# Token tensor of the second block with rows of 1152 bytes instead of 1088

## What is computed

```
meta_b = jnp.broadcast_to(meta[None].astype(x.dtype), (B, N_META, D_MODEL))
h = jnp.concatenate([meta_b, x], axis=1)
u = rms_norm(h, g_pre_mix[l])
proj = u @ w_in[l]
z_pool, v_conv, g_conv, gate_a, gate_b = jnp.split(proj, splits, axis=-1)
y_a = causal_multiscale_pool(z_pool, w_grp[l], pool_scale[l]) @ w_pool_out[l]
y_b = conformer_conv(v_conv, g_conv, w_dw[l], b_dw[l],
                     conv_ln_g[l], conv_ln_b[l]) @ w_conv_out[l]
m = jax.nn.sigmoid(gate_a) * y_a + jax.nn.sigmoid(gate_b) * y_b
h = h + rms_norm(m @ w_o[l], g_post_mix[l])
```

## Time and profile before

| | us |
|---|---|
| median of the runs shown | 2025.81 |
| the profiled execution itself | 2026.39 |
| its span in the trace | 2024.6 |
| PE busy | 2013.1 |
| DVE busy | 1513.4 |
| ACT busy | 1016.1 |

### The profile page before, as it was taken

One profiled execution on the slowest core, in us unless ns is written; L12 is line 12 of the kernel. 1 busy time (PEld: TensorE's weight loads), 2 busy tenths in 40 slices (PEclk: granted clock), 3 DMA queues, 4 the chain that ended last, 5 costly groups with the idle time before them and its releaser, 6 DMA issues.

```text
span 2024.6 us, 28913 instructions
## 1 busy us (share of the span) xinstructions
PE 2013.1 (99%) x10488; PEld 1715.0 (85%) x10488; DVE 1513.4 (75%) x2051; ACT 1016.1 (50%) x1329; POOL 82.9 (4%) x91
## 2 busy tenths in 40 slices
PE   9999999999999999999999999999999999999998
PEld 7888898888888888999888888888888888888886
DVE  6766766566756655578999856588987997898896
ACT  6645444555544544433444644454563464365353
POOL 0000102001002000002000000000000000000001
PEclk9999999999999999999999999999999999999999
DMA  9687655655667656555666566655576467467563
GB/s 348 198 202 186 177 157 172 190 175 174 179 203 243 192 190 185 175 176 159 189 195 198 178 218 185 192 173 160 190 238 195 156 208 226 146 208 235 178 209 134
DMA packets 265477, 389.33 MB, mean 192 GB/s; under 512 B 12504, under 2 KB 147032, under 8 KB 264571
## 3 DMA queue, kind: packets, MB, share of 16 engines
q1 hardware_dynamic: 262587, 377.19, 61.1%
q0 software_dynamic: 2624, 10.54, 1.9%
q10 hardware_dynamic: 144, 0.01, 0.0%
HBM read 385.02 MB, written 2.54 MB: 191 GB/s over the span
## 4 chain that ended last, share of the span: by engine, by line
PE 98%; SPq 1%; DMA 1%; DVE 0%; ACT 0%; issue 0%; DVEq 0%
PE acc L705 18%; PE acc L682 17%; PE acc L683 17%; PE acc L684 17%; PE acc L703 10%; PE acc L696 2%; PE acc L695 2%; PE acc L697 2%; PE aux L734 1%; PE aux L736 1%; PE aux L735 1%; PE acc L701 1%; PE acc L734 1%; PE acc L736 1%; PE acc L735 1%; PE aux L1638 1%
## 5 line engine op out<-in xcount | busy, mean ns | idle before, releaser
L536 DVE TENSOR_TENSOR low_rows<-stage_rows,high_rows 128x1024 fp32r<-128x1024 f32 x494 | 585.8, 1202 | 267.1 <-ACT high_rows L521 260.4
L521 ACT ACTIVATE high_rows<-stage_rows 128x1024 fp32r<-128x1024 f32 x494 | 506.6, 1034 | 516.1 <-PE acc L684 441.4
L521 ACT ACTIVATE w_high<-stage 128x1024 fp32r<-128x1024 f32 (+1 forms) x264 | 276.1, 1047 | 395.2 <-PE acc L705 292.9
L536 DVE TENSOR_TENSOR w_low<-stage,w_high 128x1024 fp32r<-128x1024 f32 (+1 forms) x264 | 319.9, 1220 | 173.9 <-ACT w_high L521 169.5
L705 PE MATMUL acc<-u,w_high 128*128 128x512 f32 x900 | 248.0, 394 | 0.0
L705 PE MATMUL acc<-hT,w_high 128*128 128x512 f32 x645 | 177.5, 394 | 0.0
L705 PEld LDWEIGHTS acc<-u,w_high 128*128 128x128 f32 x900 | 152.9, 189 | 19.1
L703 PEld LDWEIGHTS acc<-u,w_low 128*128 128x128 f32 x960 | 146.8, 188 | 20.5
L703 PE MATMUL acc<-u,w_low 128*128 128x256 f32 x960 | 152.4, 281 | 0.0
L682 PE MATMUL acc<-high_rows,hT 128*128 128x512 f32 x384 | 151.8, 395 | 0.0
L684 PE MATMUL acc<-high_rows,hT 128*128 128x512 f32 x384 | 149.6, 390 | 0.0
(11 more groups left out here) (451 smaller groups left out, 3690.1 us busy)
## 6 DMA issues: line engine op xcount, KB each, us to landing
stage_rows<-in_w_in SPq DMA_DIRECT2D x160, 512.0 KB, 3.7
stage<-in_w_in SPq DMA_DIRECT2D x136, 512.0 KB, 3.6
stage_rows<-in_w_down SPq DMA_DIRECT2D x128, 512.0 KB, 4.4
stage<-in_w_up SPq DMA_DIRECT2D x120, 512.0 KB, 4.5
stage_rows<-in_w_o SPq DMA_DIRECT2D x64, 512.0 KB, 4.1
stage_rows<-in_w_pool_out SPq DMA_DIRECT2D x16, 512.0 KB, 3.9
stage_rows<-in_w_conv_out SPq DMA_DIRECT2D x16, 512.0 KB, 4.4
stage_rows<-in_w_mem_kv SPq DMA_DIRECT2D x14, 512.0 KB, 10.9
```

Source lines behind the costliest of these rows:

```text
L521: act.activation(high[:, pr, k_from:kt, 0:p.cols], src[:, slot, k_from:kt, 0:p.cols], ACT.Copy).then_inc(high_done, 1)
L536: dve.tensor_tensor(low[:, pr, k_from:kt, 0:p.cols], src[:, slot, k_from:kt, 0:p.cols], high[:, pr, k_from:kt, 0:p.cols].bitcast(F32), ALU ...
```

## The change

The tensor becomes `u_wide`, with rows of WIDE = 288 tokens, 1152 bytes (9 x 128), of which the last 16 are never used. It starts 2 KB earlier, so that it ends where `uT` ended. Held tokens now start on a multiple of 128 bytes in both halves; streamed tokens start 64 bytes past one in both halves.

The 2 KB in front belong to the last feature tile of `merged_pair`, which `w_o` reads to its end. The feature tiles are therefore rotated: tile 15 lies in place 0, tile k in place k + 1, and the meta tokens of tile 15 are written later than the others, just before x_low of q = 7 (in the first slab of `glu_in`), by two DVE instructions of their own. A small class `Wide` does the rotation, so that the rest of the code still says `uT`.

```diff
+WIDE = TM + 16
-        uT = at("uT", Z + 64.0625, [P, KT, 2, TM], F32R)
+        u_wide = at("u_wide", Z + 62.0625, [P, KT, 2, WIDE], F32R)
+        class Wide:
+            def __getitem__(self, at):
+                _, k, half, cols = at
+                return u_wide[:, (k + 1) % KT, half, cols]
+        uT = Wide()
-            return Part(A["w_in_2"], col0, full, lambda k: (uT[:, k, 0, :], uT[:, k, 1, :]), ("pair_ready", 16), width=TM, stride=stride)
+            return Part(A["w_in_2"], col0, full, lambda k: (uT[:, k, 0, 0:TM], uT[:, k, 1, 0:TM]), ("pair_ready", 16), width=TM, stride=stride)
                     for q in (2 * r, 2 * r + 1):
+                        if q == 7:
+                            dve.wait_ge(s("u_high"), 16)
+                            v = tmp[:, 0, (KT - 1) * META:KT * META]
+                            link(dve.tensor_copy(uT[:, KT - 1, 0, 0:META], v))
+                            link(dve.tensor_tensor(uT[:, KT - 1, 1, 0:META], v, uT[:, KT - 1, 0, 0:META].bitcast(F32), ALU.subtract))
                         low_scaled(uT, q, 2 + q % 2, META, "g_pre_mix_2", "u_high", 0)
-                    link(dve.tensor_copy(uT[:, :, 0, 0:META], v))
-                    dve.tensor_tensor(uT[:, :, 1, 0:META], v, uT[:, :, 0, 0:META].bitcast(F32), ALU.subtract).then_inc(s("meta_ready"), 1)
+                    first = v[:, 0:KT - 1, :]
+                    link(dve.tensor_copy(u_wide[:, 1:KT, 0, 0:META], first))
+                    dve.tensor_tensor(u_wide[:, 1:KT, 1, 0:META], first, u_wide[:, 1:KT, 0, 0:META].bitcast(F32), ALU.subtract).then_inc(s("meta_ready"), 1)
```

## The result

The changed kernel takes 2029.01 us (median of 22 runs), the kernel before 2026.42 us in as many runs beside it: a ratio of 1.0013, 95% interval [1.0007, 1.0018]. That is 2.6 us more, where 2.2 us less were forecast, and it lies above the range (2021.8 to 2027.2). It is less than the 0.2% that counted as a change in the prediction's chances, but the interval leaves out 1. The profiled execution took 2028.52 us, with a span of 2026.7 against 2024.6.

What follows compares the result with a forecast made beforehand. PE was taken to bound the kernel, busy 99% of the span. Held tokens 2.5 us less 0.3 us given back by DVE, with streamed and meta tokens 0, gave 2025.81 - 2.2 = 2023.6 us; range 2021.8 to 2027.2.

Steps and rivals of the forecast that it cites:

- the prediction's chances: Whole kernel, against about 0.2% or 4 us: faster by more 0.06, slower by more 0.05, the same 0.89.
- the first term: Held tokens in conv_gates and pool_out: aligning both halves saves 3.2 ns a matmul, 2.5 us over 768 matmuls.
- a second difference: Held uT against y_pair and f_pair: a row of 1088 bytes against 1024, which the trace cannot separate from alignment.
- The bound: Held-token matmuls in conv_gates and pool_out: at worst all at 394 to 395 ns, a loss of 0.5 to 1.3 us.
- DVE's give-back: First conv_gates step: PE waits for DVE before the eighth slab, losing 0.27 us of gain, counted as 0.3.
- Streamed tokens: glu_in and pools: x_low's new start 64 bytes past a multiple of 128 costs nothing, within 1.8 us either way.
- Meta tokens: Tile 15 in glu_in: two extra DVE instructions, 0.3 to 0.7 us together, covered by slack and counted as 0.
- The rule of the two ports: Held-token loads on PE: separate ports for stream and weight load make their start irrelevant, sum 0 instead of 2.2.
- the 3.2 ns: pool_out's first step: extra time per matmul with uT held, 230.1 ns, over y_pair, 226.9 ns.
- Slower: Rival, chance 0.11: streams of glu_in and pools pay 1.8 us and held tokens bring nothing, time 2027.6.
- Nothing happens: Rival, chance 0.18: loads stay hidden, and non-1024-byte rows keep varying held-to-streamed distances; 2025.8, within 0.5 either way.
- DVE holds longer: Rival, chance 0.09: DVE holds PE beyond the first conv_gates step, up to all four, time 2024.5.

Runs made afterwards that it cites:

- x_low held thrice: Changed kernel with conv_gates and pool_out holding x_low for all three products, so the gates are wrong by the high half; one run, 2024.34 us.
- old rows' halves apart: Kernel before, with uT split into one array of 1088-byte rows for x_high and one behind it for x_low; 2029.64 us, ratio 1.0013.
- all loads off: Changed kernel with conv_gates and pool_out holding x_high for all three products, in place of x_low too; one run, 2027.91 us.
- the rotation alone: Changed kernel with rows of 1088 bytes again, keeping the rotated tiles and late meta tokens of tile 15; 2026.42 us against 2027.21, ratio 0.9997.
- the tensor 128 bytes earlier: Changed kernel with u_wide starting 128 bytes earlier, so x_high and x_low change places modulo 256; 2027.13 us, ratio to before 1.0001.
- the new ones': Changed kernel's 1152-byte rows, with u_wide split into one array for x_high and one for x_low; one run, 2027.62 us.
- seven tiles in rows of 1280 bytes: Tiles 9 to 15 in 1280-byte rows, tiles 0 to 8 in the old rows; 2024.95 us against 2027.21, then 2025.49 against 2026.44.
- everything 128 later: Kernel before with the whole arena, held tokens and streamed weights together, 128 bytes later; 2026.55 us, ratio 0.9996.

## Why the prediction was wrong

**The step that failed is the first term:** "Both halves get the property that `y_pair` and `f_pair` have", worth 2.5 us. The property that these tensors share is not a start on a multiple of 128 bytes. It is a start at the weights' place modulo 256: `y_pair` itself, moved by 128 bytes and still on multiples of 128, went from 227.0 to 232.4 ns. The change took x_high off that place in the eight tiles where it lay there and put x_low on it in all sixteen. What the right property would have been worth was read correctly (`y_pair`'s 226.9 ns is what x_low held thrice reached); what the change brought has the other sign: +2.35 us measured on the stretch for -2.5 forecast.

How the old rows come to be the cheaper mixture is open. As many loads lie on the place after the change as before (256 of 768). Before, the tiles with x_high on the place and those with it 128 off cost the same, 229.5 ns a matmul in the second `pool_out` step; the other third of the loads, x_low, lay 64 off to one side or the other. With the old rows' halves apart, whole tiles lie 64 off and cost 230.5 on one side and 232.9 on the other, so that 64 is not free; why the mixture is cheaper than either no run shows. After the change every tile has the distances 128, 128 and 0, and takes 233.2 ns, more than the 232.4 with all loads off.

Two groups of tensors that differ in several properties had been taken as a test of one of them. The prediction named rows of another length as a second difference but no third, a larger modulus, which could be worked out from `BASE` and the tensors' places.

**The bound was too narrow above.** The loss was limited to 0.5 to 1.3 us because the slowest regular form had 394 to 395 ns; the three forms rose to 395 - 397, busy 304.3 against 302.1 us. The slowest row that a trace happens to hold is no ceiling for a combination that is not in it.

**DVE's give-back (+0.3):** did not arise, since PE had become slower. Its mechanism and its size are right: with x_low held thrice PE waits for DVE in the step that the prediction named, and that step takes 22.13 us against 21.92 in a later one, whose opening matmul is 0.1 us longer, so some 0.3 us more.

**Streamed tokens (0 within 1.8):** +0.07 us, right by luck. From start to start the product of L696 lost 0.6 us and that of L695 0.2, and that of L697 took 0.9 us more; the prediction had no reason for such a balance. Other places moved the same stretch by up to 1.8 us.

**Meta tokens (0):** right. DVE in order of time, answering to the earlier trace rows:

```profile
823.38 0.17 DVE L2277 CAST u_wide<-tmp 128x16 fp32r<-128x16 f32 x1
823.59 0.18 DVE L2278 TENSOR_TENSOR u_wide<-tmp,u_wide 128x16 fp32r<-128x16 f32 x1
823.80 0.88 DVE L2197 SCALAR_TENSOR_TENSOR u_wide<-aux,params,u_wide 128x256 fp32r<-128x256 f32 x2
...
828.09 1.23 DVE L545 TENSOR_TENSOR w_low<-stage,w_high 128x1024 fp32r<-128x1024 f32 x1 [1.32 <-ACT w_high L530]
```

They take 0.17 and 0.18 us, within the 0.3 to 0.7 us allowed for both; x_low is done at 824.68, PE asks for it at 827.62, and DVE then still stands 1.32 us for ACT. With the rotation alone the time is that of before.

**The rule of the two ports.** The Trainium skill, "TensorE: Matmul & The Clock Gate", section "Step-by-step: what each phase is for", lets the weight load run beside the stream through a port of its own. As the prediction read it, the start of the held tokens could then not matter, and it set the 3.2 ns against that. The runs go with the 3.2 ns: tokens moved by 128 bytes and nothing else cost 22 us. The load itself is no longer, 188 ns with `f_pair` held at either distance; how load and stream meet in spite of the two ports no run here shows.

**The rivals.** "Slower" had the right side with the wrong mechanism: it put the price on the streams, which did not pay. "Nothing happens" came nearest in its reason, distances between held tokens and streamed weights, and missed that the new rows bring no new distances from tile to tile but, for x_high, one bad distance for good. "DVE holds longer" did not arise: in the changed kernel PE does not wait for DVE in the first step of `conv_gates`.

## What to carry to other kernels

When tokens are held and 512 columns of weights stream, compute both start addresses modulo 256 bytes, not the alignment of one of them alone; where the distance is 0 and stays so from load to load, these matmuls stand 227 ns apart, and where it is 128, about 232.4. For held weights and streaming tokens this kernel shows no such rule. A row length chosen as a multiple of 256 bytes keeps the place, for better or worse, in all tiles; an odd multiple of 128 switches it. And before a correlation between two tensors is taken as a cause, one run that moves a single offset is worth more than any number of rows that happen to agree.

## What was not expected of the hardware

- The distance modulo 256 between held and streamed start: with 128 tokens held and 512 columns streaming, 227 ns at 0, 232.4 at 128 (x_low and x_high held three times), and 22 us over the kernel when all KB-aligned token tensors are 128 off. The same two distances change nothing clear where the weights are held and `hT` or `u` streams (L705 of the kernel before, 393 to 395 ns at either).
- A mixture of places costs more than its share of loads that are off: 231.1 ns with one load of three off, 233.2 with two, 232.4 with all. Whether a switch has its own price (an estimate of 4 ns) or a load that is off lengthens the distances on both sides of it is open.
- Open: where weights are held and 272 tokens stream, the stretch took 145.2 us with the tensor 128 bytes earlier, 147.1 with the old rows' halves apart, 146.1 with the new ones', 144.8 with seven tiles in rows of 1280 bytes, and 146.5 with everything 128 later, where no distance had changed. The rule for held tokens does not cover these, and no run here isolates them.
